# Hybrid stream encoder on one core: which half of the tokens goes first in TensorE's dense products

## The chip, the cores and the metric

The kernel runs on one core of a Trainium2 chip. The metric is the device time of one execution in microseconds. The kernel before takes 2099.41 us, the median of three runs (2099.11, 2099.41 and 2710.35).

## What is computed

Two layers of a streaming encoder, for two request groups that share one set of weights: 512 tokens of new streams and 64 tokens of running streams, 576 together, with 1024 features each. All of it is float32. Cut to what matters here:

```python
def trunk(x, past, ...):
    for l in range(DEPTH):                       # 2
        m, rows = token_mix(rmsnorm(x, norm_mix[l]), ...)
        x = x + m
        f, conv_state = conv_ffn(rmsnorm(x, norm_ffn[l]), ...)
        x = x + f
    return rmsnorm(x, norm_final), new_state

def token_mix(xn, past, w_in, b_f, w_branch, w_gate, w_out):
    (a_q, a_k, a_v, i_q, i_k, i_w, b_q, b_k, b_v, c_q, c_k, c_v, c_f) = split(xn @ w_in)
    o_a, o_b, o_c = sparse attention, stick-breaking attention, forgetting attention
    branch = einsum('btnw,nwd->btnd', o, w_branch)      # 512 -> 1024, three times
    gate = sigmoid(xn @ w_gate)                         # 1024 -> 3 x 1024
    return einsum('btnd,btnd->btd', gate, branch) @ w_out

def conv_ffn(xn, ...):                                  # 1024 -> 2 x 2816 -> 1024
    h = xn @ w_up;  causal depthwise convolution of width 3
    return (silu(g) * u) @ w_down
```

## The kernel before

**Layout.** Activations stand with features in the 128 partitions and the 576 tokens in the free dimension. Each float32 operand of a large product is split into a high part and a low part (`xh`, `xl` for the normalised input, `oh`, `ol` for attention outputs, `ah`, `al` for the feed-forward's, `wh`, `wl` for weights), and a product is three matmuls: high x high, low activation x high weight, high activation x low weight.

**Units.** The weights come as a stream of units; a unit of eight blocks of 128 x 128 yields 128 output features. Two buffers of raw weights are filled by DMA (SP's queue). ACT makes the high part of each half unit (a chunk of 512 columns, line 481), DVE the low part (line 853), into a ring of four slots. PE waits for `low_done` at each chunk and adds to `chunks` when it is through, which frees the slot.

**Halves.** A matmul writes at most one PSUM bank, so the 576 tokens are two halves of 288. `dhalf[d][0]` is the last 288 columns of one bank and `dhalf[d][1]` the first 288 of the next, so that both can be read as one piece of 576. There are two such pairs, `d0` and `d1`, used in turn; `iq1_out` is a third, in the tensor `ab`. The innermost loop in `dense` (`project` and `up` call it), in `gate_blocks` and in `products` runs over half 0 and half 1, for each of the three matmuls of a block. The activations of a block `kk` are `xh[:, kk, 0:288]` and `xh[:, kk, 288:576]`. `norm_sum` issues two float32 matmuls of 288 columns, half 0 and half 1, which the trace shows as four.

**Order on PE.** It is written out by hand. In each layer: units KI, IQ0, IQ1 (the norm sum of the mixer's input within or ahead of IQ1), SMALL and the first half of Q[B]; five transposes; the rest of Q[B] with the indexer's scores between; then the mixers B, C, A. Each mixer has projections (Q, values with 512-column matmuls on lines 1593 and 1597, K), then attention scores and values with groups of `gate_blocks` of 12 to 30 matmuls in between, then the branch product (`branch_first` for output units 0 and 1, `dense` for 2 to 7). After branch A come eight output units, then the feed-forward: the first up unit, the norm sum of the feed-forward, and then all up and down units without anything else on PE. The last down unit of the program runs its halves apart (`down_half`, line 2013).

A dense stretch below means matmuls of 288 columns that follow each other with nothing else on PE.

## Time and profile before

| | |
|---|---|
| median of three runs | 2099.41 us |
| the profiled execution | 2097.79 us |
| its span in the trace | 2096.0 us |
| granted clock of TensorE, mean | 0.998 |
| PE busy | 2083.8 us, 99% |
| DVE busy | 1393.0 us, 66% |
| ACT busy | 1003.8 us, 48% |
| chain that ended last | 96% PE |
| HBM traffic | 83 GB/s over the span |

The span runs from the first to the last instruction that the trace holds. PE's busy time counts a matmul from its start to its modelled end, and matmuls overlap, so a record is longer than the distance to the next start: a 288-column matmul has a record of about 294 ns, and the starts are closer together than that. To learn what one costs, one has to divide the time between two starts by their number.

### The profile page before, as it was taken

How to read it: one execution, taken by the hardware profiler on the slowest of the kernel's cores; microseconds unless marked ns; L12 is line 12 of the kernel's file. 1: busy time of each engine (PE TensorE's matmuls, PEld its weight loads, DVE VectorE, ACT ScalarE, POOL GpSimd, SP SyncE). 2: the span in 40 equal slices, each digit the busy share in tenths (PEclk: the TensorE clock that was granted, in tenths of full speed). 3: DMA queues.
4: the chain of work that ended last, by engine and by line, in shares of the span. 5: the costliest groups of instructions: out<-in, count | busy, mean ns of one | idle time of the engine just before them, and what ended most of it. 6: DMA issues, size and time to landing. Idle time of an engine off the chain costs nothing.

```text
span 2096.0 us, 39576 instructions
## 1 busy us (share of the span) xinstructions
PE 2083.8 (99%) x15836; PEld 1972.8 (94%) x15836; DVE 1393.0 (66%) x2612; ACT 1003.8 (48%) x1635; POOL 228.6 (11%) x162
## 2 busy tenths in 40 slices
PE   9999999999999999999999999999999999999998
PEld 8888988898999999999998989889989999999998
DVE  7668657878747763676465786588787477536753
ACT  6267215646526652444352672255565366424432
POOL 0023000000031110011300220000001301001112
PEclk9999999999999999999999999999999999999999
DMA  6231223121122222222332212221212222232222
GB/s 204 77 106 41 91 85 102 52 72 52 61 81 81 88 83 92 90 80 91 91 108 81 96 41 91 82 96 56 77 51 64 79 90 80 91 91 80 90 84 94
DMA packets 53763, 175.03 MB, mean 84 GB/s; under 512 B 6720, under 2 KB 11408, under 8 KB 53632
## 3 DMA queue, kind: packets, MB, share of 16 engines
q1 hardware_dynamic: 47168, 158.88, 24.4%
q0 software_dynamic: 2688, 9.95, 1.2%
q10 hardware_dynamic: 3776, 4.34, 0.6%
q8 instruction: 96, 1.57, 0.3%
q14 instruction: 35, 0.29, 0.0%
HBM read 160.25 MB, written 12.90 MB: 83 GB/s over the span
## 4 chain that ended last, share of the span: by engine, by line
PE 96%; DVE 2%; ACT 1%; issue 0%; DMA 0%; SPq 0%; DVEq 0%
PE d L1499 63%; PE d L1547 14%; PE ab L1593 4%; PE d L1883 2%; PE d L1558 2%; PE d L1892 2%; PE ab L1822 1%; PE ab L1834 1%; PE d L1597 1%; PE ab L1871 1%; PE ab L1499 1%; PE ab L1816 1%; PE ab L1648 0%; PE d L1739 0%; PE ab L1679 0%; PE ab L1689 0%
## 5 line engine op out<-in xcount | busy, mean ns | idle before, releaser
L481 ACT ACTIVATE wh<-raw 128x512 fp32r<-128x512 f32 x548 | 345.0, 631 | 718.7 <-PE d L1499 563.6
L853 DVE TENSOR_TENSOR wl<-raw,wh 128x512 fp32r<-128x512 f32 x548 | 387.5, 709 | 284.8 <-ACT wh L481 275.9
L1499 PE MATMUL d<-xh,wh 128*128 128x288 f32 x2400 | 513.1, 294 | 0.7 <-DVE xl L866 0.4
L1499 PE MATMUL d<-xl,wh 128*128 128x288 f32 x2400 | 510.2, 293 | 0.0
L1499 PE MATMUL d<-xh,wl 128*128 128x288 f32 x2400 | 510.0, 293 | 0.0
L1499 PEld LDWEIGHTS d<-xh,wh 128*128 128x128 f32 x2400 | 382.3, 188 | 6.5 <-issue 4.7
L1499 PEld LDWEIGHTS d<-xl,wh 128*128 128x128 f32 x2400 | 382.0, 188 | 0.0
L1499 PEld LDWEIGHTS d<-xh,wl 128*128 128x128 f32 x2400 | 382.0, 188 | 0.0
L1547 PE MATMUL d<-xh,wh 128*128 128x288 f32 x768 | 173.5, 307 | 0.0
L1547 PE MATMUL d<-xh,wl 128*128 128x288 f32 x768 | 164.6, 295 | 0.0
L1547 PE MATMUL d<-xl,wh 128*128 128x288 f32 x768 | 164.3, 295 | 0.0
L1499 PE MATMUL d<-ah,wh 128*128 128x288 f32 x682 | 144.2, 292 | 0.0
L1499 PE MATMUL d<-ah,wl 128*128 128x288 f32 x682 | 144.2, 292 | 0.0
L1499 PE MATMUL d<-al,wh 128*128 128x288 f32 x682 | 144.2, 292 | 0.0
L434 POOL TENSOR_TENSOR al<-at,ah 128x576 f32 x44 | 63.6, 1445 | 644.3 <-ACT ah L780 644.3
L1547 PEld LDWEIGHTS d<-xh,wh 128*128 128x128 f32 x768 | 121.9, 189 | 11.6 <-issue 9.0
L1547 PEld LDWEIGHTS d<-xl,wh 128*128 128x128 f32 x768 | 123.1, 188 | 0.0
L1547 PEld LDWEIGHTS d<-xh,wl 128*128 128x128 f32 x768 | 123.1, 188 | 0.0
L1398 DVE TENSOR_TENSOR hb<-d,rstd 128x512 f32<-128x512 f32 x88 | 60.9, 692 | 78.5 <-PE d L1499 78.5
L1409 DVE SCALAR_TENSOR_TENSOR cv<-hb,pr,cv 128x578 f32<-128x578 f32 x88 | 72.3, 821 | 58.5 <-ACT cv L771 58.5
L1499 PEld LDWEIGHTS d<-ah,wl 128*128 128x128 f32 x682 | 108.2, 187 | 0.0
L1499 PEld LDWEIGHTS d<-ah,wh 128*128 128x128 f32 x682 | 108.2, 187 | 0.0
(323 smaller groups left out, 3268.9 us busy)
## 6 DMA issues: line engine op xcount, KB each, us to landing
raw<-in_w SPq DMA_DIRECT2D x286, 512.0 KB, 3.5
out_o_k<-k POOLq DMA_DIRECT2D x4, 1152.0 KB, 7.6
out_o_v<-v POOLq DMA_DIRECT2D x4, 1024.0 KB, 8.8
x<-in_xT SPq DMA_DIRECT2D x8, 288.0 KB, 5.5
k<-in_bc_k_past ACTq DMA_DIRECT2D x4, 512.0 KB, 4.6
v<-in_bc_v_past ACTq DMA_DIRECT2D x4, 512.0 KB, 5.7
out_y<-z SPq DMA_DIRECT2D x4, 432.0 KB, 2.7
raw<-in_w SPq DMA_DIRECT2D x4, 256.0 KB, 6.0
```

Source lines behind the costliest of these rows:

```text
L434: pool.tensor_tensor(al[:, bass.ds(i, 1), :].rearrange("p a n -> p (a n)"), at[:], ah[:, bass.ds(i, 1), :].rearrange("p a n -> p (a n)").b ...
L481: act.activation(wh[:, c % SPLIT_SLOTS, :], stored, ACT.Copy).then_inc(high_done, 1)
L853: dve.tensor_tensor(lows, stored, highs, ALU.subtract).then_inc(low_done, 1)
L1398: dve.tensor_tensor(hb[:, s, 2:514], hv[:, 0:512], rstd[:, 0:512], ALU.mult)
L1409: dve.scalar_tensor_tensor(cv[:, s, :], hb[:, s, 1:T + 3], pr[:, bass.ds(R_CW + CONV * row + 1, 1)], cv[:, s, :], ALU.mult, ALU.add).then_ ...
L1499: ins = pe.matmul(outs[half], w_, r_[:, kk, HALF * half:HALF * half + HALF], start=first and n == 0 and begin, stop=last and n == len(kks) ...
L1547: ins = pe.matmul(dhalf[d][half], w_, r_[:, kk, HALF * half:HALF * half + HALF], start=first and kk == 0, stop=last and kk == KD - 1)
L1558: ins = pe.matmul(dhalf[(d + j) % 2][half], weights[:, (c + j) % SPLIT_SLOTS, kk * P:kk * P + P], heads[:, kk, HALF * half:HALF * half + H ...
L1593: pe.matmul(o, x_[:, kk, t * P:t * P + P], w_[:, c % SPLIT_SLOTS, cols:cols + n], start=first and f_ and starts(t), stop=last and l_, skip ...
L1597: ins = pe.matmul(src(4), xp[:, kk, :], w_[:, c % SPLIT_SLOTS, cols:cols + n], start=first and f_ and starts(4), stop=last and l_, skip_gr ...
L1883: ins = pe.transpose(spare[:, o + n:o + n + P], w1[:, a + n:a + n + P], ident)
L1892: pe.matmul(spare[r, t * P:(t + 1) * P], val(2 * p + i, kt), w2[:, w:w + P], start=first, stop=kt == t, skip_group_check=True)
```

## The change

`dense`, `project`, `project_half`, `gate_blocks` and `up` get a parameter `order`, a function that gives for block `kk` the order of the two halves. `straight` is half 0 first, as before and by default; `swapped` is half 1 first; `swapped_later` is straight for the blocks 0 to 3 and swapped for 4 to 7. The same matmuls run with the same operands into the same places. The semaphore increments stay on the last matmul of a chunk, which in a swapped unit is that of half 0. The first matmul of an accumulation in each half still starts it.

Where it is swapped: in layer 0 the unit IQ0 and blocks 0 and 1 of IQ1, up to the norm sum; in layer 1 the unit IQ1, SMALL and the first half of Q[B], behind the norm sum; in mixer B the second half of K[B]+2, K[B]+3 and the first four gate blocks; from output unit 2 of each branch product on, until the next attention part (the Q[C] units, the K[C] units and four gate blocks of C; the Q[A] units; the eight output units and the first up unit). Q[A]+3 is swapped in its second half, with the four gate blocks behind it. Behind the feed-forward's norm sum the order is straight again.

```diff
-            def dense(before, lo_wait, c0, outs, rh, rl, kks, begin=True, end=True, behind=no_wait):
+            def straight(kk):
+                return 0, 1
+
+            def swapped(kk):
+                return 1, 0
+
+            def swapped_later(kk):
+                return (0, 1) if kk < 4 else (1, 0)
+
+            def dense(before, lo_wait, c0, outs, rh, rl, kks, begin=True, end=True, behind=no_wait, order=straight):
...
                     for w_, r_, first, last in ((hi_w, rh, True, False), (hi_w, rl, False, False), (lo_w, rh, False, True)):
-                        for half in range(2):
+                        for half in order(kk):
                             ins = pe.matmul(outs[half], w_, r_[:, kk, HALF * half:HALF * half + HALF],
...
-            def project(l, u, d, wait=no_wait):
+            def project(l, u, d, wait=no_wait, order=straight):
                 pe.wait_ge(dfree[d % 2], freed(l, d))
-                dense(l * CHUNKS, wait, 2 * u, dhalf[d % 2], xh, xl, range(KD))
-
-            def project_half(l, u, d, b):
+                dense(l * CHUNKS, wait, 2 * u, dhalf[d % 2], xh, xl, range(KD), order=order)
+
+            def project_half(l, u, d, b, order=straight):
...
-            def gate_blocks(l, m, h, blocks):
+                dense(l * CHUNKS, no_wait, 2 * u + b, dhalf[d % 2], xh, xl, range(4 * b, 4 * b + 4), b == 0, b == 1, order=order)
+
+            def gate_blocks(l, m, h, blocks, order=straight):
...
                     for w_, r_, first, last in ((hi_w, xh, True, False), (hi_w, xl, False, False), (lo_w, xh, False, True)):
-                        for half in range(2):
+                        for half in order(kk):
                             ins = pe.matmul(dhalf[d][half], w_, r_[:, kk, HALF * half:HALF * half + HALF],
...
             for l in range(LAYERS):
                 project(l, U_KI, D_KI, xn_wait(l, 0))
-                project(l, U_IQ, D_IQ0)
+                project(l, U_IQ, D_IQ0, order=straight if l else swapped)
                 if l == 0:
                     def first_sum(kk):
...
-                    dense(l * CHUNKS, no_wait, 2 * (U_IQ + 1), iq1_out, xh, xl, range(KD), behind=first_sum)
+                    def swapped_first(kk):
+                        return (1, 0) if kk < 2 else (0, 1)
+                    dense(l * CHUNKS, no_wait, 2 * (U_IQ + 1), iq1_out, xh, xl, range(KD), behind=first_sum, order=swapped_first)
+                    order = straight
                 else:
                     norm_sum(1 + 2 * l)
-                    dense(l * CHUNKS, no_wait, 2 * (U_IQ + 1), iq1_out, xh, xl, range(KD))
+                    order = swapped
+                    dense(l * CHUNKS, no_wait, 2 * (U_IQ + 1), iq1_out, xh, xl, range(KD), order=order)
...
-                project(l, U_SMALL, D_SMALL)
-                project_half(l, U_Q[B], D_Q[B], 0)
+                project(l, U_SMALL, D_SMALL, order=order)
+                project_half(l, U_Q[B], D_Q[B], 0, order)
...
-                        project(l, U_K[B] + 2, D_K[B] + 2)
-                        project(l, U_K[B] + 3, D_K[B] + 3)
+                        project(l, U_K[B] + 2, D_K[B] + 2, order=swapped_later)
+                        project(l, U_K[B] + 3, D_K[B] + 3, order=swapped)
...
                             if p == 0:
 
-                                gate_blocks(l, m, 0, range(0, 4))
+                                gate_blocks(l, m, 0, range(0, 4), swapped)
                                 pe.wait_ge(dfree[1 - gate_bank(m)], freed(l, D_G[m] + 1))
                                 logits_x(p)
                                 gate_blocks(l, m, 0, range(4, 8))
...
                         if m == C:
                             for j in range(4):
-                                project(l, U_Q[C] + j, D_Q[C] + j)
+                                project(l, U_Q[C] + j, D_Q[C] + j, order=swapped)
                             project_values(C)
                             pe.wait_ge(past_c, 32 * (l + 1))
-                            project(l, U_K[C], D_K[C])
-                            project(l, U_K[C] + 1, D_K[C] + 1)
+                            project(l, U_K[C], D_K[C], order=swapped)
+                            project(l, U_K[C] + 1, D_K[C] + 1, order=swapped)
...
                             scores_wide(0)
                             scores_next(0)
-                            project(l, U_K[C] + 2, D_K[C] + 2)
-                            project(l, U_K[C] + 3, D_K[C] + 3)
-                            gate_blocks(l, m, 0, range(0, 4))
+                            project(l, U_K[C] + 2, D_K[C] + 2, order=swapped)
+                            project(l, U_K[C] + 3, D_K[C] + 3, order=swapped)
+                            gate_blocks(l, m, 0, range(0, 4), swapped)
...
-                            project(l, U_Q[A], D_Q[A])
-                            project(l, U_Q[A] + 1, D_Q[A] + 1)
-                            project(l, U_Q[A] + 2, D_Q[A] + 2)
+                            project(l, U_Q[A], D_Q[A], order=swapped)
+                            project(l, U_Q[A] + 1, D_Q[A] + 1, order=swapped)
+                            project(l, U_Q[A] + 2, D_Q[A] + 2, order=swapped)
...
                             scores_wide(0)
                             scores_next(0)
-                            project(l, U_Q[A] + 3, D_Q[A] + 3)
-                            gate_blocks(l, m, 0, range(0, 4))
+                            project(l, U_Q[A] + 3, D_Q[A] + 3, order=swapped_later)
+                            gate_blocks(l, m, 0, range(0, 4), swapped)
...
                     for j in range(2, KD):
                         d = D_BR[m] + j
                         pe.wait_ge(dfree[d % 2], freed(l, d))
-                        dense(l * CHUNKS, no_wait, 2 * U_BR[m] + j, dhalf[d % 2], oh, ol, range(4))
+                        dense(l * CHUNKS, no_wait, 2 * U_BR[m] + j, dhalf[d % 2], oh, ol, range(4), order=swapped)
 
                 for j in range(KD):
-                    project(l, U_OUT + j, D_OUT + j, xn_wait(l, 1) if j == 0 else no_wait)
-
-                def up(f, i, s, wait=no_wait):
+                    project(l, U_OUT + j, D_OUT + j, xn_wait(l, 1) if j == 0 else no_wait, order=swapped)
+
+                def up(f, i, s, wait=no_wait, order=straight):
                     pe.wait_ge(dfree[s], START + l * (D_USES // 2) + f * (D_HALF // 2) + i + D_UP // 2)
-                    dense(l * CHUNKS + f * (2 * U_HALF) + 4 * i, wait, 2 * U_UP + 2 * s, dhalf[s], xh, xl, range(KD))
+                    dense(l * CHUNKS + f * (2 * U_HALF) + 4 * i, wait, 2 * U_UP + 2 * s, dhalf[s], xh, xl, range(KD), order=order)
...
                 for f in range(2):
                     if f == 0:
-                        up(f, 0, 0, xn_wait(l, 2))
+                        up(f, 0, 0, xn_wait(l, 2), swapped)
                         norm_sum(2 + 2 * l)
                         up(f, 0, 1)
```

No instruction moves against another kind of instruction: DVE, ACT, POOL and SP have the same rows in the same order. On PE the order of rows is the same as well, since a row names the tensor and not the half. Here is PE at the norm sum of layer 0's mixer, before:

```order
L1499 MATMUL ab<-xh,wh 128x288 [waits low_done]
L1499 MATMUL ab<-xh,wh 128x288
L1499 MATMUL ab<-xl,wh 128x288 x2
L1499 MATMUL ab<-xh,wl 128x288 x2
L1499 MATMUL ab<-xh,wh 128x288 x2
L1507 MATMUL ab<-sumsq,cf 128x288 [waits acc_ready,s_const]
L1507 MATMUL ab<-sumsq,cf 128x288
L1499 MATMUL ab<-xh,wh 128x288 x2
```

and with the change:

```order
L1508 MATMUL ab<-xh,wh 128x288 [waits low_done]
L1508 MATMUL ab<-xh,wh 128x288
L1508 MATMUL ab<-xl,wh 128x288 x2
L1508 MATMUL ab<-xh,wl 128x288 x2
L1508 MATMUL ab<-xh,wh 128x288 x2
L1516 MATMUL ab<-sumsq,cf 128x288 [waits acc_ready,s_const]
L1516 MATMUL ab<-sumsq,cf 128x288
L1508 MATMUL ab<-xh,wh 128x288 x2
```

An "x2" is the pair of halves. Ahead of the rows of `sumsq` (the norm sum) it was half 0, half 1 and is now half 1, half 0; behind them it is half 0, half 1 in both. The waits stand where they stood.

The second place is PE behind the values of mixer C, where the K[C] units begin, with the change:

```order
L1606 MATMUL d<-wh,xp 128x512
L1606 MATMUL d<-wl,xp 128x512
L1508 MATMUL d<-xh,wh 128x288 [waits low_done,dfree0,past_c]
L1508 MATMUL d<-xh,wh 128x288
L1508 MATMUL d<-xl,wh 128x288 x2
L1508 MATMUL d<-xh,wl 128x288 x2
```

The first matmul of 288 columns, which carries the waits, is now that of half 1; before, it was that of half 0.

## Rows read from the trace of the kernel before

**Rows 1.** The page: busy time, granted clock, the gate blocks' line

```profile
PE 2083.8 (99%) x15836; PEld 1972.8 (94%) x15836; DVE 1393.0 (66%) x2612; ACT 1003.8 (48%) x1635; POOL 228.6 (11%) x162
...
PEclk9999999999999999999999999999999999999999
...
L1547 PE MATMUL d<-xh,wh 128*128 128x288 f32 x768 | 173.5, 307 | 0.0
```

**Rows 2.** Waits: who waited for whom, us, times, longest

```profile
ACT wh L481 <- PE d L1499: 563.6, 346, 5.8
...
PE ab L1606 <- DVE av L1018: 1.7, 1, 1.7
...
PE d L1499 <- DVE xl L866: 0.4, 1, 0.4
```

**Rows 3.** Line 1499, feed-forward of layer 0: duration ns min/median/max, first and last start

```profile
L1499 PE MATMUL d<-xh,wh x720: 288/292/509, 641.0 to 1058.7; 128*128 128x288 f32 x180
...
L1499 PE MATMUL d<-xh,wl x720: 291/292/293, 641.8 to 1059.2; 128*128 128x288 f32 x180
```

**Rows 4.** Line 1499, last mixer stretch of layer 0

```profile
L1499 PE MATMUL d<-xh,wl x144: 292/294/302, 583.2 to 640.1; 128*128 128x288 f32 x144
L1499 PE MATMUL d<-oh,wh x48: 292/294/302, 563.5 to 582.0; 128*128 128x288 f32 x48
```

**Rows 5.** Windows: PE, PEld, DVE, ACT, POOL busy (x), clock, DMA, GB/s

```profile
563.00:640.00 77.00, 77.00 (x579) 77.00 (x578) 41.23 (x61) 26.26 (x42) 27.14 (x17) 1.00 0.24 76
641.00:1059.00 418.00, 418.00 (x3216) 417.95 (x3215) 252.45 (x477) 190.62 (x263) 54.64 (x38) 1.00 0.29 89
```

**Rows 6.** PE's timeline, norm sum of layer 0's feed-forward: start, us

```profile
640.27 1.13 PE L1507 MATMUL ab<-sumsq,cf 128*128 128x288 f32 x4
```

**Rows 7.** Line 1499 before and behind the first norm sum

```profile
L1499 PE MATMUL d<-xh,wl x32: 292/295/302, 7.7 to 21.2; 128*128 128x288 f32 x32
...
L1499 PE MATMUL d<-xh,wl x24: 291/292/293, 29.1 to 37.8; 128*128 128x288 f32 x24
```

**Rows 8.** Norm sum of layer 1's mixer (timeline), and line 1499 behind it

```profile
1059.32 1.13 PE L1507 MATMUL ab<-sumsq,cf 128*128 128x288 f32 x4
...
L1499 PE MATMUL d<-xh,wl x24: 292/294/302, 1067.2 to 1076.1; 128*128 128x288 f32 x24
L1499 PE MATMUL ab<-xh,wh x16: 292/295/508, 1060.1 to 1066.0; 128*128 128x288 f32 x16
```

**Rows 9.** Line 1499, branch B and the Q[C] units

```profile
L1499 PE MATMUL d<-xh,wl x64: 292/294/302, 247.1 to 272.1; 128*128 128x288 f32 x64
```

**Rows 10.** Behind the values: K[C] and its gate blocks, then layer 1

```profile
L1499 PE MATMUL d<-xl,wh x32: 291/292/293, 298.6 to 310.4; 128*128 128x288 f32 x32
...
L1547 PE MATMUL d<-xh,wl x8: 291/292/295, 327.0 to 329.5; 128*128 128x288 f32 x8
...
L1499 PE MATMUL d<-xl,wh x32: 291/292/293, 1336.9 to 1348.8; 128*128 128x288 f32 x32
```

**Rows 11.** Timeline of the last unit, its halves apart

```profile
2076.62 0.29 PE L2013 MATMUL d<-ah,wh 128*128 128x288 f32 x1
...
2081.02 0.29 PE L2013 MATMUL d<-ah,wh 128*128 128x288 f32 x1
...
2083.26 0.29 PE L2013 MATMUL d<-ah,wl 128*128 128x288 f32 x1
```

**Rows 12.** Line 1499, K[B]+2 and K[B]+3

```profile
L1499 PE MATMUL d<-xl,wh x32: 292/294/302, 110.9 to 123.0; 128*128 128x288 f32 x32
```

**Rows 13.** Line 1499, the Q[A] units behind branch C

```profile
L1499 PE MATMUL d<-xh,wl x48: 292/294/302, 443.7 to 462.3; 128*128 128x288 f32 x48
```

**Rows 14.** Line 1499, layer 1's last mixer stretch

```profile
L1499 PE MATMUL d<-xh,wl x144: 292/294/302, 1621.6 to 1678.5; 128*128 128x288 f32 x144
```

**Rows 15.** Chain that ended last, end of mixer B: start, us

```profile
195.81 0.92 ACT w L615
...
220.88 6.66 PE d L1558 x48
```

1 line of the change is left out of this document (removed).

## Prediction, made before the changed kernel was run

> **What bounds the kernel now.** I read the busy shares and the slices first: PE is busy for 2083.8 of 2096.0 us, in every slice of 40 but the last at nine tenths or more, at the full granted clock [rows 1]. The reader should see that nothing but PE's own time is left to win. The waits come next: PE's own waits are four rows from 1.7 down to 0.4 us, 4.1 together, while ACT waits 563.6 us for PE before it makes a new high part of the weights [rows 2]. So the weights stand ready, the suppliers wait for PE, and a matmul that costs less shortens the span, as long as the suppliers keep up.
>
> Then I asked for one line, the 288-column matmuls of `dense`, in stretches without any other PE instruction. In the feed-forward part of layer 0 there are 3216 of them [rows 5], from 641.0 to 1059.2 us: 418.2/3215 = **130.1 ns from start to start**, and no record but the first is longer than 293 ns [rows 3]. In the last stretch of the mixers just before it, 576 matmuls of the same shape run from 563.5 us to the norm sum at 640.27 us: 76.77/576 = **133.3 ns**, with records up to 302 ns [rows 4, 6]. The granted clock is 1.00 in both, and neither has idle PE time [rows 5]. So the same instruction has two paces, 3.25 ns apart, and each lasts as long as the stretch does. I call them the fast and the slow pace; a longest record of 293 or of 302 ns tells them apart at a glance.
>
> What sets the pace? Three readings. First, the pace changes where something stands between two dense stretches. In front of the norm sum of layer 0's feed-forward the pace is slow, behind it fast [rows 3, 4]. At the first norm sum it is also slow before (302) and fast after (293) [rows 7]. At the norm sum of layer 1's mixer it is the other way round: the fast feed-forward stands before it, and the 120 matmuls behind run from 1060.1 to 1076.1 us with records of 302 ns [rows 3, 8]. The norm sum's records read the same where it ends a slow pace and where it ends a fast one (1.13 us [rows 6, 8]), so it does not *make* a pace, it *exchanges* the two. That is how a hidden step that alternates from matmul to matmul would look, if the norm sum shifts it by one against the alternation of the two halves. Second, the values part (512-column matmuls) exchanges them as well: slow in front of it [rows 9], fast behind [rows 10]. Third, the last unit of the program runs one half by itself. From 2076.62 to 2081.02 us half 0 alone takes 4.40/33 = 133.3 ns each, from 2081.02 to 2083.26 half 1 alone takes 2.24/17 = 131.8 ns [rows 11]. A half alone meets the hidden step in both positions by turns and comes out between or at the slow pace. All this fits one rule: **the pace is fast when half 0 falls on one position of a two-step alternation and slow when it falls on the other**, and half 0 and half 1 do not cost the same. Which position it is I can't read; that there are two, I can.
>
> **The change, term by term.** It adds and removes no instruction, wait or transfer on any engine. It exchanges which half goes first. Where the changed order begins, one half stands twice in a row; from there every matmul of the stretch stands on the other position. By the rule, each stretch whose order differs from before takes the other pace, and the others keep theirs, because the number of matmuls ahead of them is unchanged.
>
> Slow stretches that get the new order, in matmuls (48 for a full unit, 6 for one block of `kk`):
> - layer 0: unit IQ0 and two blocks of IQ1, 48 + 12 = 60 (the first stretch [rows 7]);
> - layer 1: IQ1, SMALL and half of Q[B], 48 + 48 + 24 = 120 [rows 8];
> - per layer in B: the second half of K[B]+2, K[B]+3, four gate blocks, 24 + 48 + 24 = 96; now slow [rows 12];
> - per layer: branch B from j = 2 and the four Q[C], 144 + 192 = 336 [rows 9];
> - per layer: branch C and three Q[A], 144 + 144 = 288; half of Q[A]+3 and four gate blocks, 48; slow [rows 13];
> - per layer: branch A, the output units and the first up unit, 144 + 384 + 48 = 576 [rows 4]; layer 1 repeats it [rows 14].
>
> That is 180 + 2 x (96 + 336 + 288 + 48 + 576) = 2868 matmuls x 3.25 ns (76.77/576 less 418.2/3215) = **-9.3 us**.
>
> One group goes the wrong way. The four K[C] units and the four gate blocks of C, 192 + 24 = 216 per layer, are fast now, with records of 293 ns, 295 at most [rows 10], and they get the new order too. By the rule they turn slow: 2 x 216 x 3.25 = **+1.4 us**. The reason against this is that after a break the pace might be set anew by whatever starts; the norm sums, which exchange and don't reset, are the nearest rows, so I take the rule. A kept fast pace (0) is the other bound.
>
> The seams: about six per layer where one half follows itself. A matmul behind its own half costs 133.3 ns at most in the last unit [rows 11], so a seam costs 3 ns against the fast pace and nothing against the slow one; 16 seams are below 0.1 us. Without a row that shows a single seam I keep 0 to 0.2 us.
>
> Does the gain reach the end? The high and low parts of the weights come from ACT and DVE. In the last mixer stretch DVE is busy 41.23 of 77 us and ACT 26.26; in the feed-forward, where PE already runs at the fast pace, PE has not one idle microsecond [rows 5]. So a pace of 130 ns is fed there, and the mixers' stretches ask no more of the ring than that. The narrow place is the end of mixer B: the chain that ended last leaves PE for ACT's `w` at 195.81 us and comes back over DVE at 220.88 [rows 15]. It left PE later than the stretch that is shortened (two units from 110.9 to 123 us [rows 12] and four gate blocks), so it starts earlier by the same amount; were DVE behind on its own account there, 2 x 96 x 3.25 = 0.6 us would be lost. I cost that at nothing and keep it for the range.
>
> Sum: -9.3 + 1.4 + 0.1 = -7.8 us, made against the profiled execution (2097.79 us, a span of 2096.0 and 1.8 around it), so 2090.0; the median of the runs shown is 1.6 us above that execution, so the same step on the median gives 2099.4 - 7.8 = **2091.6 us**.
>
> Here a page speaks against the change. The rows say that one shape at one granted clock has two paces, 130.1 and 133.3 ns [rows 3, 4]. The Trainium skill, in "TensorE: Matmul & The Clock Gate", section "Wait — 56ns, not 53.3ns?", gives the distance of back-to-back matmuls as the columns over the clock plus about 2.5 ns, with no word on which output or which operand came before; for 288 columns an estimate from it is 122.5 ns for every one. By that rule the order of halves is worth nothing, and the sum would be 0. The trace doesn't agree with its figure at either pace.
>
> **Rivals.**
> - *All of it fast*, 18%: as forecast, but the K[C] stretches keep the fast pace, because what starts behind the 512-column matmuls starts in step. For it: every stretch that starts behind them is fast, in both layers [rows 10]. Against it: each came from a slow one. -9.3 + 0.1 = -9.2 us: 2090.2.
> - *The order is no cause*, 13%: the pace hangs on something that the program's two halves don't touch, say the count of instructions in the queue, and the norm sum's exchange has another source. Then the same stretches stay slow: 2099.4, between 2099.0 and 2099.8. For it: no row shows a swap inside a stretch. Against it: two matmuls of one half in a row do change the cost [rows 11]. The page named above would have this outcome.
> - *Part of it*, 12%: stretches that begin behind a break don't take the exchange, or fall back behind the next wait, as short gate groups of 24 may. The long ones are 2 x (336 + 288 + 576) = 2400 matmuls or 7.8 us; less the 1.4 of K[C] that leaves -6.4, and if they hold for half their length -2.5. Around 2095.
> - *Slower*, 6%: only the group that is fast now changes. A stretch in the slow pace may be where the engine comes to rest from any order (the first K[B]+2 unit starts behind a short block and ends there [rows 12]), while the fast pace has to be met exactly. Then the swap repairs nothing and K[C] falls to the slow pace: +1.4 and 0.1 for seams, 2100.9. It decides from the point where fewer than 432 of the 2868 slow matmuls leave that pace.
>
> **How the numbers follow.** The forecast has 51%. It and the first rival, with their bounds (seams 0.2, DVE 0.6, 0.3 for the noise of the median), lie between 2089.5 and 2092.6; gate blocks behind a swap may change pace with it though their order is as before: of the 3 x 768 on their line [rows 1] 2160 keep the order, and a quarter of those at 3.25 ns is 1.8 us, which widens it down to 2087.5. The partial case reaches to 2097.5. From 2087.5 to 2097.5 lies 81%; the no-cause case and the slower one are left out. The most that any case moves is 12 us, 0.6%. About 2% is what the verdict here counts as a change, so within 2% gets 0.98, and 0.01 each side is for what I have not thought of.
>
> **What would show it.** In the changed kernel's rows for the long mixer stretches: no record above about 293 to 297 ns, and 130 ns from start to start over the 576 matmuls ahead of the feed-forward's norm sum (74.9 us, not 76.8). Behind that norm sum the feed-forward must still be fast; if it turns slow, the rule on exchanges is wrong and the loss (3216 matmuls [rows 5] x 3.25 = 10.5 us in layer 0 alone) would eat the whole gain. Records of 302 ns in K[C] show the wrong-way term. The prediction is wrong if the swapped stretches still show 302, or if PE's own waits grow from 4.1 us by what was gained.

## The result and the profile after

The changed kernel takes 2120.3 us (median of 4 runs, 2119.58 to 2120.53) against 2099.47 for the kernel before in the same comparison (median of 4; one of its runs took 2710.35 us, for which no trace has a cause): a ratio of 1.010, interval 1.0088 to 1.0113. That is 20.8 us more, where 7.8 less were forecast and the range ended at 2097.5. The profiled execution has a span of 2118.3 us, 22.3 above that of before; the granted clock is 1.00 in every stretch below, which is the upper level of 2.4 GHz.

Cut both spans at the norm sums, where the mixer and the feed-forward of each layer meet. The columns are length, busy time and instructions of PE, granted clock, DMA share, GB/s. The kernel before:

```profile
0.00:640.27 640.27, 637.14 (x4798) 1.00 0.27 85
640.27:1059.32 419.05, 419.05 (x3222) 1.00 0.29 88
1059.32:1678.63 619.31, 618.55 (x4689) 1.00 0.24 76
1678.63:2083.39 404.76, 404.76 (x3111) 1.00 0.27 85
```

The changed kernel:

```profile
0.00:641.23 641.23, 637.13 (x4797) 1.00 0.27 84
641.23:1070.99 429.76, 429.76 (x3222) 1.00 0.28 86
1070.99:1690.81 619.82, 619.03 (x4690) 1.00 0.25 76
1690.81:2105.74 414.93, 414.93 (x3111) 1.00 0.27 83
```

The differences are +0.96, **+10.71**, +0.51 and **+10.17** us, 22.35 together, which is the whole of it. The mixers, where the order was changed, barely move. The loss lies in the two feed-forward parts, of whose matmuls only the first unit (48 of some 3200, ahead of the norm sum and so in the window before) was touched.

What answers to [rows 3], the feed-forward of layer 0, and the same line in layer 1 (duration ns min/median/max, first and last start):

```profile
L1508 PE MATMUL d<-xh,wh x720: 292/295/510, 642.0 to 1070.3; 128*128 128x288 f32 x180
L1508 PE MATMUL d<-xh,wl x720: 292/294/302, 642.7 to 1070.9; 128*128 128x288 f32 x180
...
L1508 PE MATMUL d<-xh,wl x688: 292/294/302, 1692.3 to 2037.2; 128*128 128x288 f32 x172
```

The longest record behind the first is now 302 ns where it was 293: the slow pace, 429.76/3222 = 133.4 ns. Next what answers to [rows 4], then to [rows 9], to [rows 10] and to the second line of [rows 7]:

```profile
L1508 PE MATMUL d<-xh,wl x144: 292/295/302, 584.2 to 641.1; 128*128 128x288 f32 x144
L1508 PE MATMUL d<-oh,wh x48: 292/294/302, 564.4 to 583.0; 128*128 128x288 f32 x48
...
L1508 PE MATMUL d<-xh,wl x64: 292/294/302, 247.4 to 272.4; 128*128 128x288 f32 x64
...
L1508 PE MATMUL d<-xl,wh x32: 292/295/302, 298.9 to 311.0; 128*128 128x288 f32 x32
...
L1508 PE MATMUL d<-xh,wl x24: 292/294/302, 29.2 to 38.1; 128*128 128x288 f32 x24
```

None of the slow stretches that got the new order became fast: the 576 matmuls ahead of the norm sum still take 76.8 us (564.4 to 641.23). The fast stretches turned slow: K[C], 0.69 us in layer 0 (216 matmuls from 298.61 to 330.59 us, before from 298.31 to 329.60), and the first stretch behind the first norm sum. These two are small, and as the section on the state shows, they also turn out either way in the kernel before; the feed-forward does not. The norm sum reads as in [rows 6], and the windows that answer to [rows 5] show that nothing else is behind it:

```profile
641.23 1.13 PE L1516 MATMUL ab<-sumsq,cf 128*128 128x288 f32 x4
```

```profile
564.00:641.00 77.00, 77.00 (x580) 77.00 (x579) 41.27 (x61) 26.27 (x42) 27.15 (x17) 1.00 0.24 76
642.00:1070.00 428.00, 428.00 (x3211) 427.95 (x3210) 249.27 (x477) 190.62 (x263) 54.85 (x38) 1.00 0.28 86
```

PE has no idle time in the feed-forward, as before; DVE and ACT are as busy as before; PE's waits over the program, the last two of which follow, are 5.3 us together against 4.1.

```profile
PE d L1508 <- DVE xl L866: 0.9, 2, 0.5
PE d L1508 <- DVE wl L851: 0.7, 1, 0.7
```

So no supply ran short. The same instructions cost 3.3 ns more each.

### The profile page after: what moved, and what is told of

The parts are those of the page before. It is cut to its first block, busy times and chain, and to the rows that moved or that the text cites. A ratio compares the mean times of both kernels' runs of the same rounds, so it can differ in the third digit from the quotient of the medians.

```text
span 2118.3 us, 39576 instructions
## 1 busy us (share of the span) xinstructions
PE 2105.2 (99%) x15836; PEld 1995.0 (94%) x15836; DVE 1387.1 (65%) x2612; ACT 1004.1 (47%) x1635; POOL 229.1 (11%) x162
## 4 chain that ended last, share of the span: by engine, by line
PE 97%; DVE 2%; ACT 1%; issue 0%; DMA 0%; SPq 0%; DVEq 0%
PE d L1508 64%; PE d L1556 14%; PE ab L1602 4%; PE d L1896 2%; PE d L1567 2%; PE d L1905 2%; PE ab L1835 1%; PE ab L1847 1%; PE d L1606 1%; PE ab L1508 1%; PE ab L1884 1%; PE ab L1829 1%; PE ab L1661 0%; PE d L1752 0%; PE ab L1692 0%; PE ab L1702 0%
## 5 line engine op out<-in xcount | busy, mean ns | idle before, releaser
L1508 PEld LDWEIGHTS d<-al,wh 128*128 128x128 f32 x682 | 109.7, 189 | 0.0
```

Source lines behind the costliest of these rows:

```text
L1508: ins = pe.matmul(outs[half], w_, r_[:, kk, HALF * half:HALF * half + HALF], start=first and n == 0 and begin, stop=last and n == len(kks) ...
```

## The experiments

The theory, as it stood after the first runs: the pace of a stretch does not follow from its own order. It is decided at the place where something else (norm sum, values part, short matmul) stands between two stretches, and lasts until the next such place. The rivals were the prediction's rule of exchanges, a loss that needs the whole new order of the mixers, and later a cause inside the halves' addresses.

### One unit alone

The kernel before, with only the first up unit swapped, the last ahead of the norm sum:

```diff
-                        up(f, 0, 0, xn_wait(l, 2))
+                        up(f, 0, 0, xn_wait(l, 2), swapped)
```

> The kernel before, with one unit per layer changed: the first up unit, which stands directly ahead of the feed-forward's norm sum, runs half 1 first; behind the norm sum half 0 is first as before. My theory now (call it the pull): in a slow stretch the engine is pulled into the slow position whatever the order, so the swap ahead of the norm sum repairs nothing, and the norm sum exchanges the position against the half; swapping on one side of it alone makes the exchange miss, and the whole feed-forward turns slow. Expected: feed-forward of layer 0 at 133.3 ns per matmul, records up to 302 ns, 3216 x 3.25 = 10.5 us and in layer 1 3054 x 3.25 = 9.9 us more, together +20 us against before, about 2119.5. Rival (the long swap): it is the swap far ahead in the mixers that spoils the feed-forward; then one unit of 48 matmuls does nothing, 2099.5.

2119.39 us against 2098.54: 1.0097 (1.008 to 1.0114), the whole loss, from 48 matmuls per layer. Its feed-forward rows in layer 0:

```profile
L1505 PE MATMUL d<-xh,wl x720: 292/294/302, 643.1 to 1071.2; 128*128 128x288 f32 x180
```

The longest record is 302 ns, as in the changed kernel. What the mixers' order does before that unit plays no part.

### The order given back one unit early

The changed kernel, with the last output unit and the first up unit straight again:

```diff
-                    project(l, U_OUT + j, D_OUT + j, xn_wait(l, 1) if j == 0 else no_wait, order=swapped)
+                    project(l, U_OUT + j, D_OUT + j, xn_wait(l, 1) if j == 0 else no_wait, order=swapped if j < KD - 1 else straight)
...
-                        up(f, 0, 0, xn_wait(l, 2), swapped)
+                        up(f, 0, 0, xn_wait(l, 2))
```

> The changed kernel, but straight again from the last output unit on, so that 96 matmuls in the order half 0, half 1 stand ahead of the feed-forward's norm sum. The pull: feed-forward fast again, -20.4 us against the changed kernel; what stays is the K[C] groups (432 matmuls, slow) and layer 0's 108 matmuls behind the first norm sum, (432 + 108) x 3.25 = +1.8 us over before: 2101.2. Rival (the long swap): still 2120. Rival (my first rule): the mixers would be fast, 2092.

2099.12 us against 2098.54 (1.0004, 0.9994 to 1.0013): the whole loss of the feed-forward is gone. What is left, 0.6 us, is less than the 1.8 expected; the section on the state says why. Feed-forward of layer 0:

```profile
L1508 PE MATMUL d<-xh,wl x720: 291/292/293, 642.5 to 1059.9; 128*128 128x288 f32 x180
```

Records end at 293 again. The swapped 480 matmuls ahead of it are still slow (76.8 us for the 576), so swapping a long stretch repairs nothing.

### The new order kept over the norm sum

If the norm sum exchanges two positions, it should not matter which half comes first as long as the order is the same on both sides. The changed kernel, with every unit of the feed-forward swapped as well:

```diff
-                            up(f, i, s)
+                            up(f, i, s, order=swapped)
...
-                        dense(l * CHUNKS + f * (2 * U_HALF), wait, 2 * U_DOWN + 3 * j, dhalf[d % 2], ah, al, range(FH))
+                        dense(l * CHUNKS + f * (2 * U_HALF), wait, 2 * U_DOWN + 3 * j, dhalf[d % 2], ah, al, range(FH), order=swapped)
```

> The changed kernel with the swapped order kept behind the norm sum, through all up and down units of the feed-forward. The pull with an exchange at the norm sum that does not care which half is first: feed-forward fast, about 2101, and a same-half seam where the next layer's KI unit starts straight. Rival (half 0 has to come first behind a norm sum for the fast pace): feed-forward slow, 2120.

2120.06 us against 2098.54 (1.0102, 1.0085 to 1.0119). Slow:

```profile
L1508 PE MATMUL d<-xl,wh x720: 288/294/302, 642.4 to 1070.5; 128*128 128x288 f32 x180
```

The expectation of an exchange that does not care which half leads is refuted. The halves are not alike.

### Short cases behind the program's end

22 cases of some 80 matmuls each, with the operands of the kernel and five transposes ahead of each, so that a start can be seen by itself. The frame of a case, with the norm sum between:

```diff
+            for kk in range(6):  # ahead
...
+                    for half in (0, 1):
...
+            pe.matmul(norm_out[0], cf[:, C_ONE:C_ONE + P], sumsq[:, HALF * 0:HALF * 0 + HALF], start=True, stop=True)
+            pe.matmul(norm_out[1], cf[:, C_ONE:C_ONE + P], sumsq[:, HALF * 1:HALF * 1 + HALF], start=True, stop=True)
+            for kk in range(8):  # behind
```

> The kernel before with 22 short cases appended on PE after all results are finished, about 250 us more; only the pace of each is read. Each case starts with five float32 transposes (after which a stretch was slow everywhere), 36 matmuls ahead, something between, and 48 or more behind. Expected by the pull: control slow (133.3 ns, records up to 302); a same-half seam in the slow pace gives some ten matmuls without a stall and then slow again; norm sum between straight and straight: fast (130.0, records up to 293); straight to swapped over the norm sum: slow; swapped on both sides: fast; a swapped stretch ahead and straight behind: slow; two norm sums in a row: slow (exchanged twice). Open, with no forecast: what a seam does to the fast pace; whether one float32 matmul, one or two or fourteen 512-column ones, or a single short one exchange the paces; whether the outputs' place in their banks or the tokens' place in SBUF makes the two halves different. If halves differ by the place in the bank, cases with both outputs at bank starts have one pace only.

The case that should have copied the kernel, a norm sum with the order kept, came out slow:

```profile
L2074 PE MATMUL d<-xh,wl x16: 292/294/302, 2128.1 to 2133.8; 128*128 128x288 f32 x16
```

So a norm sum does not by itself turn slow into fast. A 128-column matmul in its place did, and fourteen 512-column ones did. Where the two outputs stand in their bank made no difference (302 at bank starts and ends). With both halves reading the same tokens the records behind the first few never passed 298, but the pace was 133.3 ns all the same. The number of matmuls ahead is not what differs: the last case has the same 36 ahead of its norm sum (behind it the outputs stand at bank starts) and came out fast, 130.0 ns. The distances, below, tell the two apart.

### A seam in the fast pace

The kernel before, with the down units of the first feed-forward part of layer 0 swapped:

```diff
-                        dense(l * CHUNKS + f * (2 * U_HALF), wait, 2 * U_DOWN + 3 * j, dhalf[d % 2], ah, al, range(FH))
+                        dense(l * CHUNKS + f * (2 * U_HALF), wait, 2 * U_DOWN + 3 * j, dhalf[d % 2], ah, al, range(FH), order=swapped if l == 0 and f == 0 else straight)
```

> The kernel before, with the down units of the first feed-forward part of layer 0 (eight units of 66 matmuls, 528 in all) swapped and everything else straight, so that two seams stand inside the fast stretch. If the fast pace is held by alternation alone (my first rule): the 528 matmuls slow, +1.7 us, and fast again behind. If the slow pace pulls (now): slow from the first seam to the norm sum of layer 1, 528 + 1584 matmuls and the KI and IQ0 units, 2208 x 3.25 = +7.2 us. If a seam harms only a slow stretch: +0.

2105.01 us against 2097.74 (1.0035, 1.0023 to 1.0048): +7.3, as expected if the slow pace is where the engine comes to rest. Line 1505 up to the first seam, and behind the second seam, where the order is straight again:

```profile
L1505 PE MATMUL d<-xh,wl x336: 290/292/293, 641.4 to 771.8; 128*128 128x288 f32 x168
...
L1505 PE MATMUL d<-xl,wh x384: 289/295/303, 842.6 to 1065.9; 128*128 128x288 f32 x192
```

One seam ends the fast pace, and a second one, back to the old order, does not bring it back. A shift between two positions would have.

### A unit ahead of the values, and a short matmul ahead of the norm sum

Two edits of the kernel before that leave the order of the disputed stretches alone. The last Q[C] unit swapped:

```diff
-                                project(l, U_Q[C] + j, D_Q[C] + j)
+                                project(l, U_Q[C] + j, D_Q[C] + j, order=swapped if j == 3 else straight)
```

> The kernel before, with only the last Q[C] unit swapped, ahead of the values part of mixer C; K[C] behind it straight as before. The position theory: a swapped stretch reaches the values part at another place of its cycle of four matmuls, so the K[C] units and gate blocks of C (216 per layer) turn slow, records up to 302, +1.4 us in all, though their own order is untouched. Rival (what counts is only that half 0 comes first behind): they stay fast, records up to 295.

One 64-column matmul ahead of the last output unit, no order changed at all:

```diff
+                    if j == KD - 1:
+                        nudge(l, D_OUT + j, 64)
```

> The kernel before, every order straight, with one 64-column matmul more per layer ahead of the last output unit (its result is overwritten by the unit itself). It only moves the place in the cycle of four at which the norm sum arrives. The position theory: slow stretches have a stall (a distance of 140 ns) behind every second matmul of half 0; a norm sum that comes three matmuls behind the last stall leads to the fast pace, one that comes one behind leads to the slow pace. Whichever it is here, the feed-forward must follow it, layer by layer: 10.5 and 9.9 us are at stake. Rival (the order of halves decides): fast in both layers, as before.

The first, 2099.23 us in one run against 2097.74, which is within the spread of the kernel before (2097.44 to 2099.26); K[C], untouched, is slow:

```profile
L1505 PE MATMUL d<-xh,wl x32: 292/294/302, 298.9 to 311.1; 128*128 128x288 f32 x32
```

That line alone proves little, for K[C] is slow in other traces too. This one is of the kernel with three short matmuls far behind K[C] (told below), which is the kernel before up to there:

```profile
L1499 PE MATMUL d<-xl,wh x32: 292/294/302, 298.4 to 310.5; 128*128 128x288 f32 x32
```

Of the nine traces whose program is that of the kernel before up to the K[C] units of layer 0, five show them fast and four slow. What the swapped unit adds is read from the distances in the next section.

The second, 2119.49 us in one run against 2097.74: two matmuls of 196 ns cost 21.8 us, because both feed-forwards turn slow:

```profile
L1526 PE MATMUL d<-xh x2: 196/196/196, 627.5 to 1677.3; 128*128 128x64 f32 x2
...
L1499 PE MATMUL d<-xl,wh x720: 291/295/303, 641.6 to 1069.7; 128*128 128x288 f32 x180
```

The loss therefore needs no swap. What counts is the state in which the norm sum is met.

### What the state is

The distances from start to start, worked out from the starts in the traces, show it. In the slow pace they are not evenly long: 131, 131, 132 and **140** ns in turn, now and then 1 ns less (533 or 534 for the four, 133.3 to 133.4 each), and the stall of 140 stands behind every second matmul of the costly half, half 0 (a row doesn't name its half; it follows from the program's order). The record of 302 ns is that of the matmul ahead of the stall. In the fast pace they are 132 and 128 in turn. A swap inside the slow pace is followed by some ten to fourteen matmuls without a stall, and then by the cycle again, with its stall behind half 0 as before. The last five distances ahead of the norm sum, and those from the first matmul behind it on (ns; the norm sum's own are left out):

```
before, layer 0        132 140 130 131 132 | 349 125 132 128      fast
before, layer 1 mixer  129 131 129 131 133 | 348 132 133 131      slow (met in the fast pace)
changed, layer 0       131 132 140 130 135 | 346 132 131 132 140  slow
first up unit alone    131 131 140 131 135 |                      slow
64 columns ahead       131 131 132 141 130 | 348 132 133 131      slow
changed, layer 1 mixer 131 140 131 131 132 | 345 126 128 133 133  slow (half 1 first behind)
```

The norm sum is followed by the fast pace where it comes three matmuls behind the last stall, and by the slow one at one or two behind. A swapped unit ends on half 0 instead of half 1, so the stall can't stand three ahead. The traces of all the kernels here, short cases apart, have 32 norm sums that are met in the slow pace with half 0 first on both sides (and the activations in their old place): 24 at three behind, all followed by the fast pace, and 8 at one behind, all by the slow one. With half 1 first behind it, three is not the place: that is the last row of the table.

The values part has the opposite place. With half 0 first ahead of it, K[C] was fast in 7 of 18 cases, each time at one behind the last stall, and slow in 11, each time at three. Behind a swapped unit (the unit alone, the changed kernel, and the two kernels made from it) the values part is met at two, four or none behind, and K[C] was slow in 8 of 8.

The place is not fixed by the program. The first norm sum of layer 0 has the same instructions ahead of it in ten traces; it came at three behind in four of them (fast), at one behind in five (slow), and once in the fast pace (slow). The trace of before has all the parts that go either way fast, and its execution (2097.79 us) is faster than any of the four timed runs it is compared by (from 2099.11). That accounts for the kernel with the order given back: its K[C] units and first stretch are slow in its trace, 1.8 us over an execution with all of them fast. By the shares counted here an average execution of the kernel before already carries an estimated 1.1 of these (0.7 x 4/9 + 0.7 x 7/9 + 0.35 x 6/10), which leaves 0.7; measured were 0.6.

39 more short cases varied the place and the tokens that the halves read:

```diff
+            pe.matmul(ab[:, 2, 0:128], wh[:, 0, 0:P], xh[:, 0, 0:128], start=True, stop=True)
...
+                        pe.matmul(dhalf[0][half], w_, r_[:, kk % 8, off32[half][0]:off32[half][1]], start=kk == 0 and n == 0, stop=kk == 12 - 1 and n == 2)
```

> The kernel before with 39 short cases appended on PE after all results are finished; only paces are read. Each begins with five transposes and a straight stretch of 36 or 42 matmuls, so that what stands between arrives at two places of the cycle; between: two, one or four float32 matmuls of 288 columns, one float32r matmul of 32, 64, 128, 256 or 512 columns, fourteen of 512. Position theory: for two float32 matmuls the outcome goes with the place (three behind a stall: fast, one behind: slow), and some of the others have a place of their own that leads to the fast pace. A seam in a fast stretch: slow behind it by the pull. Last, 12 blocks whose two halves read tokens from the same or from other offsets: if the place of the tokens in SBUF makes the halves differ, two halves from token 0 and two from token 288 have different paces, and pairs of equally aligned tokens have none of the stalls of 140 ns; if not, all read alike.

In this order: behind a 128-column matmul met at three behind the stall, behind one met at one behind, behind a norm sum met at three behind, and then both halves from token 0 and both from token 32:

```profile
L2139 PE MATMUL d<-xl,wh x16: 292/292/293, 2180.6 to 2186.2; 128*128 128x288 f32 x16
...
L2337 PE MATMUL d<-xl,wh x14: 292/295/303, 2360.9 to 2365.9; 128*128 128x288 f32 x14
...
L2308 PE MATMUL d<-xl,wh x16: 291/292/293, 2334.5 to 2340.1; 128*128 128x288 f32 x16
...
L2458 PE MATMUL d<-xl,wh x24: 294/295/298, 2475.8 to 2484.7; 128*128 128x288 f32 x24
...
L2476 PE MATMUL d<-xl,wh x24: 292/294/297, 2495.9 to 2504.7; 128*128 128x288 f32 x24
```

Of the single 128-column matmuls met in the slow pace with half 0 first, four at three behind were fast and five at one behind slow. Fourteen 512-column matmuls do the reverse: fast at one behind, slow at three. Having 36 or 42 matmuls ahead did not choose the place as it was meant to: either number led to either. The last two lines differ in the tokens alone: from token 0 a matmul costs 133.4 ns, from token 32 it costs 131.7. Tokens 16, 64, 128 and 256 also gave 133.3 to 133.4, tokens 160 and 288 gave 131.6 to 131.7. (All are means from the ninth matmul on.) With four bytes a token and `xh` at 34944 in the partition (128 above a multiple of 256), the cheap starts are those at a multiple of 256 bytes. Half 1 (1152 bytes on) has one, half 0 has not. That is the difference of [rows 11], 133.3 for half 0 and 131.8 for half 1, with its cause.

### The halves' addresses in the kernel

The kernel before, with its activations moved on by 128 bytes (what stands behind them moves by 256, so its place modulo 256 stays), no instruction changed:

```diff
+        sb("shift", [P, 32])
         xh = sb("xh", [P, KD, T], F32R)
...
+        sb("shift_back", [P, 32])
```

> The kernel before with all orders straight and all its instructions; only the activation tensors (xh, xl, oh, ol, ah, al and what shares their space) stand 128 bytes further in SBUF, so that half 0 starts at 0 modulo 256 bytes and half 1 at 128, where it was the other way round. Address theory: what I called half 0 is the half that starts at 128 modulo 256, so the stall of 140 ns now stands behind half 1, the norm sum arrives behind a stalled or an even place, as it did behind swapped units, and both feed-forwards turn slow: +20 us with no order changed. Rival (the halves differ by their order or by the output bank): 2098.5.

The same, with half 1 first everywhere, which puts the aligned half in its old place in the order:

```diff
-                        for half in range(2):
+                        for half in (1, 0):
```

> The same shift, and in addition half 1 first in every dense, gate and branch matmul. Address theory: order and addresses are both turned, so the first half of each pair again starts at 128 modulo 256, and the paces are those of the kernel before: feed-forward fast, about 2098.5. Rival: an order of its own, slow, about 2119.

The shift alone: 2120.25 us against 2098.33 (1.0105, 1.009 to 1.012). The shift and the swap: 2098.97 (1.0004, 0.9995 to 1.0014). Feed-forward of layer 0, of the one and of the other:

```profile
L1501 PE MATMUL d<-xl,wh x720: 292/294/302, 642.1 to 1070.2; 128*128 128x288 f32 x180
```

```profile
L1501 PE MATMUL d<-xl,wh x720: 291/292/293, 641.9 to 1059.4; 128*128 128x288 f32 x180
```

Moving the data by 128 bytes does the same harm as the change, and the swap then undoes it, except that the K[B] units, which are fast in all thirteen traces with the old addresses, are slow in both kernels with the new ones (96 matmuls per layer, 0.6 us in all; the values part ahead of them reads the moved activations too). In the feed-forward it is the half's start address that gives it its place in the cycle, and not its number.

### Using it

If the place decides, one short matmul at the right place should turn the slow stretches fast: behind branches C and A (288 and 480 matmuls per layer), with a third one that hands the feed-forward's norm sum the place that it needs. They stand ahead of the third unit of branches C and A, and ahead of the last output unit:

```diff
+            def nudge(d):
+                pe.matmul(dhalf[d % 2][0][:, 0:P], tri[:, 0:P], tri[:, 0:P], start=True, stop=True, skip_group_check=True)
...
+                        if j == 2 and m != B:
+                            nudge(d)
...
+                        nudge(D_OUT + j)
```

> The kernel before, all orders straight, with three 128-column matmuls more per layer whose results are overwritten: ahead of output unit 2 of branch C, of output unit 2 of branch A, and of the last output unit ahead of the feed-forward. In the short cases such a matmul turned a slow stretch fast whenever it came three matmuls behind a stall, and a fast stretch slow. Both branch places stood at three behind a stall in every trace so far. Expected: 288 matmuls behind branch C and 144 + 336 behind branch A at 130.0 ns, the third nudge brings the slow pace back for 96 matmuls so that the norm sum meets the place that makes the feed-forward fast: 2 x 768 x 3.25 = 5.0 us less six nudges of 0.12 = 4.3 us faster than before. Rival (the place differs in the real stretch from that in the short cases): some stretch stays slow; if the norm sum then comes at the wrong place, +20 us.

The same with the third one ahead of the first up unit:

> The same, with the third nudge one unit later, ahead of the first up unit, so that only 48 slow matmuls stand ahead of the norm sum. 2 x 816 x 3.25 = 5.3 us less 0.7 = 4.6 us faster if the place at the norm sum is again three behind a stall (48 and 96 are both multiples of four, so it should be); +20 us if not.

Both missed: 2098.95 us each against 2098.52 (1.0002, 0.9993 to 1.0011; 1.0003, 0.9994 to 1.0012). The stretch behind branch C in the first of them stayed slow:

```profile
L1499 PE MATMUL d<-ol,wh x48: 292/294/302, 424.9 to 443.4; 128*128 128x288 f32 x48
```

The place was right: each of these short matmuls came three behind a stall. But the distances at them, which read `tri` at 32 bytes above a multiple of 256, were 58 + 190 ns. In the short cases that turned fast, they were 64 + 184. So the third version gives the short matmul the alignment that it had there, its stationary operand on a multiple of 256 and its moving one 128 above:

```diff
-                pe.matmul(dhalf[d % 2][0][:, 0:P], tri[:, 0:P], tri[:, 0:P], start=True, stop=True, skip_group_check=True)
+                pe.matmul(dhalf[d % 2][0][:, 0:P], tri[:, 56:56 + P], tri[:, 24:24 + P], start=True, stop=True, skip_group_check=True)
```

> The kernel with three nudges per layer (ahead of output unit 2 of branches C and A, and of the last output unit), where the nudge's operands now start where they did in the short cases, by SBUF address modulo 256 bytes: the stationary one at 0, the moving one at 128 (before it was 32 for both, and a nudge cost 58 + 190 ns and left the slow pace, against 64 + 184 ns and the fast pace in the short cases). If the pace depends on the start addresses modulo 256: the stretches behind branches C and A fast, the third nudge slow again, and a gain of 5.0 - 0.7 = 4.3 us. If the output's bank is what differed: no change again, 2098.9. If the norm sum is met at the wrong place: +20 us.

**2094.16 us** against 2098.33 (0.9979, 0.997 to 0.9988): 4.2 us less, where 4.3 were expected, and the fastest kernel of this study. The stretches behind branch A and behind branch C:

```profile
L1499 PE MATMUL d<-xh,wl x112: 291/292/293, 582.6 to 625.6; 128*128 128x288 f32 x112
...
L1499 PE MATMUL d<-ol,wh x47: 291/292/293, 425.0 to 442.9; 128*128 128x288 f32 x47
```

No record of these lines passes 293 where the kernel before has 302 [rows 4]. Both operands of the short matmul were moved at once, so which of the two has to stand right is not shown.

## Why the prediction was wrong

- **The bound** was read rightly: PE's own time and nothing else. PE's waits went from 4.1 to 5.3 us, and DVE at the end of mixer B cost nothing that shows.
- **Two paces, 130.1 and 133.3 ns, told apart by 293 and 302**: right, and every later reading rests on it.
- **The step that failed** is the rule: "each stretch whose order differs from before takes the other pace, and the others keep theirs, because the number of matmuls ahead of them is unchanged". Both halves of it are false. The slow pace is a cycle of four with one stall, which settles itself on the costly half from either order, so a swap inside it repairs nothing (the given-back order, the seam). The fast pace is entered only at a break that is met at one place of that cycle (three behind a stall for the norm sum, one for the values part), so an untouched stretch depends on what stands ahead of it (the single unit, the 64 columns). Nor does the number of matmuls ahead fix that place: with the same program ahead, K[C] of layer 0 was fast in five traces and slow in four. The norm sum does not exchange paces. Ahead of the feed-forward it was met at the one place that leads to fast, and behind the feed-forward it was met in the fast pace, which leads to slow. Two such meetings look like an exchange, and I took them for one. The trace of before had the distances that could have told the two apart; I read medians and longest records only.
- **-9.3 us for 2868 matmuls**: measured 0; the 576 matmuls take 76.8 us in both kernels. The price itself was slightly off: 76.77/576 less 418.2/3215 is 3.20 ns and not 3.25, which makes it -9.2.
- **+1.4 us for K[C]**: 0.69 us in layer 0 against the trace of before, the size forecast (0.7 per layer), which is luck in part. K[C] is slow because the values part is met at the wrong place, whatever its own order (it is so with the one unit ahead of the values swapped), and the trace of before happens to have K[C] fast in both layers, the only one to do so of the nine traces with the old order and addresses there.
- **0 for the feed-forward**: +10.7 and +10.2. The prediction named this outcome, with its size (10.5 us in layer 0), as the sign that would refute it, and gave it no chance. It stood on one reading of three norm sums. A case that is priced at 20 us and rests on that belongs among the rivals. The rival called "slower" had the mechanism half right (the slow pace is where the engine comes to rest, and the fast one has to be met exactly), and stopped at K[C] without asking what else is entered through such a meeting.
- **"The order is no cause"** falls too: one unit's order is worth 20.9 us. By the rule of the Trainium skill, "TensorE: Matmul & The Clock Gate", section "Wait — 56ns, not 53.3ns?", every one of these matmuls would take an estimated 122.5 ns; none of the paces in any run is that, and the distances within a stretch, behind its first two matmuls and apart from waits, ran from 125 to 141 ns.
- The range took in only cases that gain; the one without an effect and the one that loses (2100.9) were left outside, and neither comes near 2120. It is the rule that needed a chance against it.

## What to carry to other kernels

Where one shape of matmul shows two paces at one granted clock, look at the distances from start to start ahead of each place where the pace changes, not at means. A swap, an added instruction or a moved buffer ahead of such a place can cost or give 2.5% of the dense stretch behind it, and a kernel that is tuned around it stays fast only as long as nobody touches the last instructions ahead of the break. Look at the start address of the moving operand as well: a move of 128 bytes was worth 22 us here. And compare several executions before an unchanged stretch is said to have changed, for some of them go either way by themselves.

## What the runs showed of the hardware

- A 288-column matmul of this kernel whose moving operand starts on a multiple of 256 bytes costs 131.6 to 131.7 ns, and 133.3 to 133.4 at the starts tried off it (128 or 192 above), if both halves start alike. Alternating 0 and 128 above gives 130.0 or 133.4, so a mix can be better than the better of them alone. In the short cases 0 and 192 above gave 132.5, and 128 and 192 above 132.2.
- Both paces are stable over thousands of matmuls, and only the slow one was reached again after every seam that was tried.
- What comes between is followed by one or the other by its place in the cycle, and its own operands' alignment counts as well (58 + 190 ns stayed slow, 64 + 184 turned fast).
- One program's executions differ in it: K[C] of layer 0, some 0.7 us, was fast in five of nine traces with the same program ahead, and the stretch behind the first norm sum, 0.35 us, in four of ten. The norm sum ahead of the feed-forward was met at three behind a stall in each of the nine traces with the old addresses in which the feed-forward of layer 0 is fast.

What inside the engine makes the cycle of four is not settled, nor is what makes one execution reach a break at another place than the next. That both halves could be put on a multiple of 256 bytes in the kernel itself (other lengths of the halves, or a gap between them) was not tried.
